# Two stacked transformer blocks with experts: the row sums of an expert move between the next expert's gate and up products, the sums signal by halves, the next layer's weights wait for them, and the last norm reads PSUM

## The reference, cut to what matters

```
for l in range(DEPTH):                      # DEPTH = 2
    h = rms_norm_2(x, norm1_g[l]) * (1 + scale1) + shift1
    proj = h @ w_in[l] + b_in[l]            # w_in: 1024 x 4880
    ...                                     # mixers, merged
    x = x + gate1 * (merged @ w_out[l])
    h2 = rms_norm_2(x, norm2_g[l]) * (1 + scale2) + shift2
    x = x + gate2 * hierarchical_moe(h2, ...)
return rms_norm_2(x, final_norm_g)

# hierarchical_moe, for each of 32 experts e (weights of 2 MB each):
a = t @ w_gate[e]                           # 1024 x 512
u = t @ w_up[e]                             # 1024 x 512
out = out + (silu(a) * u * combine[:, e]) @ w_down[e]   # 512 x 1024
```

## Time and profile before

| what | value |
|---|---|
| median of 3 runs | 2452.65 us (2448.65 to 2454.6) |
| the profiled execution's own time | 2453.15 us |
| its span on the core | 2451.5 us |
| TensorE busy | 91% of the span |
| VectorE, ScalarE, POOL busy | 44%, 24%, 2% |
| DMA, mean | 265 GB/s over the span |
| chain that ended last | PE 67%, DMA 18%, DVE 10%, ACT 3%, issue 1% |

### The profile page before, as it was taken

How to read it: one execution, slowest core, us unless ns; L and a number is a source line. 1 busy time by engine, 2 the same in 40 slices (tenths; PEclk the granted TensorE clock), 3 DMA queues, 4 the chain that set the end, 5 groups by cost and what they waited for, 6 DMA issues and landing times.

```text
span 2451.5 us, 31925 instructions
## 1 busy us (share of the span) xinstructions
PE 2229.5 (91%) x12988; PEld 1455.5 (59%) x12988; DVE 1085.4 (44%) x2397; ACT 589.0 (24%) x1304; POOL 58.4 (2%) x88
## 2 busy tenths in 40 slices
PE   8999999999999999999998987878799999987776
PEld 7888869946865798467764433333568744433332
DVE  4764458883464688543433222222325342222222
ACT  4331523001243220031622111111314422111111
POOL 0010000001000000002000000000002000000000
PEclk9999999999999999999998999998899989999998
DMA  8221244496933645835248999999843469999996
GB/s 304 103 78 69 86 146 165 175 369 206 330 111 116 230 159 205 338 131 172 103 196 361 427 427 428 427 428 427 337 143 111 201 245 428 427 428 427 428 427 295
DMA packets 141054, 650.66 MB, mean 265 GB/s; under 512 B 6986, under 2 KB 13434, under 8 KB 116320
## 3 DMA queue, kind: packets, MB, share of 16 engines
q1 hardware_dynamic: 138480, 641.47, 66.5%
q0 software_dynamic: 2416, 7.02, 1.2%
HBM read 647.16 MB, written 1.31 MB: 265 GB/s over the span
## 4 chain that ended last, share of the span: by engine, by line
PE 67%; DMA 18%; DVE 10%; ACT 3%; issue 1%; DVEq 0%; ACTq 0%
PE ps L106 64%; DMA wring<-in_w_up 11%; DMA AR<-in_w_up 7%; PE ps L109 3%; DVE wring L129 2%; DVE AR L125 2%; ACT AR L115 1%; DVE AR L129 1%; ACT L115 1%; ACT HT L115 1%; DVE wring L125 1%; DVE AR L120 1%; DVE AR L133 0%; ACT wring L115 0%; DVE XN L121 0%
## 5 line engine op out<-in xcount | busy, mean ns | idle before, releaser
L106 PE MATMUL ps<-HT,wring 128*128 128x256 f32 (+1 forms) x2848 | 532.9, 345 | 5.0 <-DVE wring L125 4.0
L106 PEld LDWEIGHTS ps<-HT,wring 128*128 128x128 f32 x2848 | 467.0, 193 | 63.1 <-issue 6.6
L106 PE MATMUL ps<-wring,AR 128*32 128x512 f32 (+3 forms) x1312 | 334.8, 601 | 16.8 <-DVE AR L125 15.7
L106 PE MATMUL ps<-wring,MN 128*32 128x512 f32 (+1 forms) x1376 | 218.9, 643 | 50.8 <-DMA wring<-in_w_up 38.9
L115 ACT ACTIVATE AR<-ps 128x128 f32<-128x128 f32 (+6 forms) x234 | 94.6, 404 | 707.7 <-PE ps L106 651.7
L106 PEld LDWEIGHTS ps<-wring,AR 128*32 128x32 f32 (+1 forms) x1312 | 132.2, 150 | 172.8 <-issue 171.8
L125 DVE TENSOR_TENSOR AR<-ps,AR 128x512 f32<-128x512 f32 (+4 forms) x200 | 100.6, 503 | 261.9 <-ACT AR L115 164.3
L106 PE MATMUL ps<-AR 128*128 128x128 f32 (+6 forms) x1368 | 198.5, 414 | 13.4 <-DVE AR L125 11.0
L106 PEld LDWEIGHTS ps<-wring,MN 128*32 128x32 f32 (+1 forms) x1376 | 66.5, 124 | 194.2 <-issue 103.3
L141 DVE COPY HT<-ps 128x512 f32<-128x512 f32 x64 | 44.3, 692 | 301.1 <-PE ps L106 301.1
L106 PEld LDWEIGHTS ps<-AR 128*128 128x128 f32 (+4 forms) x1368 | 137.1, 176 | 49.8 <-issue 37.4
(11 more groups left out here) (176 smaller groups left out, 2146.3 us busy)
## 6 DMA issues: line engine op xcount, KB each, us to landing
wring<-in_w_up SPq DMA_DIRECT2D x40, 2048.0 KB, 40.8
wring<-in_w_gate SPq DMA_DIRECT2D x38, 2048.0 KB, 41.3
wring<-in_w_down SPq DMA_DIRECT2D x38, 2048.0 KB, 45.4
wring<-in_w_ada SPq DMA_DIRECT2D x24, 2048.0 KB, 11.8
wring<-in_ffn_w_up SPq DMA_DIRECT2D x20, 2048.0 KB, 8.1
AR<-in_w_down SPq DMA_DIRECT2D x20, 2048.0 KB, 45.4
AR<-in_w_gate SPq DMA_DIRECT2D x20, 2048.0 KB, 36.8
wring<-in_w_in SPq DMA_DIRECT2D x18, 2048.0 KB, 10.0
```

What stands on the lines that cost most here:

```text
L106: return Ins(self.eng and self.eng.matmul(out, lhs, rhs, start=start, stop=stop), None)
```

## The change

Four edits, all in the second block.

1. **Order in an expert.** `scatter(ex - 1)` stands between the gate and the up product of `ex`, no longer behind both. `up` is split for that. The fold of the gate's rows signals by itself (`tg`), and the buffer of these rows is freed by that signal.
2. **The sums signal by halves.** The last scatter signals after m = 0 (`first`) and after m = 1 (`end`). `after_join` no longer waits for `join_mm`; `summed(e, layer, m)` waits for the half that the next operation reads.
3. **Weights of layer 1.** SP waits for the end of layer 0's last scatter before it issues `qk1`, and so before all that stands behind it; `qk0` is issued as before.
4. **The last norm.** ScalarE squares both halves of a row straight from PSUM (`final_root`), VectorE adds them, makes the factor and scales from PSUM into `X` (`final_part`); the copies to `X` and VectorE's own square are gone. SP stores four pieces of 256 KB, each as soon as its half is scaled.

```
@@ sync
+                if layer and name == "qk1":
+                    e.wait_ge(sig("join_mm0"), "end")
                 weights((name, layer), win[:, c0:c0 + n], 8, n)
...
         for m in range(2):
-            e.wait_ge(sig("last_v"), ("final", m, 1))
-            e.dma_start(out[0, 128 * m:128 * m + 128, :], X[:, m, :]).then_inc(dma("out"))
+            for c in range(2):
+                h = slice(512 * c, 512 * c + 512)
+                e.wait_ge(sig("last_v"), ("final", m, c))
+                e.dma_start(out[0, 128 * m:128 * m + 128, h], X[:, m, h]).then_inc(dma("out"))
@@ tensor
...
             for ex in range(32):
-                up(ex)
+                up("gate", ex)
                 if ex:
                     scatter(ex - 1)
+                up("eup", ex)
                 inner(ex)
...
-                if ex == 31:
-                    ins.then_inc(sig(f"join_mm{layer}"), "end")
+                    if ex == 31:
+                        ins.then_inc(sig(f"join_mm{layer}"), "end" if m else "first")
@@ vector
+        def final_part(m):
+
+            done, act = sig("norm_v"), sig("norm_a")
+            tag = ("final", m)
+            r, y, z, f = sm((*tag, "r"), 2), sm((*tag, "y"), 1), sm((*tag, "z"), 1), sm((*tag, "f"), 1)
+            v.wait_ge(act, (*tag, "square", 1))
+            v.tensor_scalar(r[:, 1:2], r[:, 1:2], 1e-6, None, ADD).then_inc(done, (*tag, "sum"))
+            v.wait_ge(act, (*tag, "square", 0))
+            v.tensor_tensor(f, r[:, 0:1], r[:, 1:2], ADD).then_inc(done)
+            v.wait_ge(act, (*tag, "root"))
+            v.reciprocal(z, y).then_inc(done)
+            v.scalar_tensor_tensor(f, z, f, z, MUL, MUL).then_inc(done)
+            v.tensor_scalar(f, f, -0.5, 1.5, MUL, ADD).then_inc(done)
+            v.tensor_tensor(f, z, f, MUL).then_inc(done)
+            v.wait_ge(dma("fn"), "final")
+            for c in range(2):
+                h = slice(512 * c, 512 * c + 512)
+                v.scalar_tensor_tensor(X[:, m, h], PA[("moe", 1), m, c][:, :], f, MG[:, h], MUL, MUL).then_inc(sig("last_v"), (*tag, c))
@@ scalar
             table()
             for m in range(2):
+                summed(a, layer, m)
                 tag, key = ("moe", layer), (sig("norm_a"), ("last", layer, m))
+                if layer:
+                    final_root(m)
+                    continue
...
+        def final_root(m):
+
+            done = sig("norm_a")
+            tag = ("final", m)
+            r, y = sm((*tag, "r"), 2), sm((*tag, "y"), 1)
+            for c in (1, 0):
+                a.activation(XN[:, m, c * 512:c * 512 + 512], PA[("moe", 1), m, c][:, :], ACT.Square, scale=1.0 / 32,
+                             accum_out=r[:, c:c + 1]).then_inc(done, (*tag, "square", c))
+            a.wait_ge(sig("norm_v"), (*tag, "sum"))
+            a.activation(y, r[:, 0:1], ACT.Sqrt, bias=r[:, 1:2]).then_inc(done, (*tag, "root"))
@@ all
     def after_join(e, layer):
 
-        for name in ("mm", "v", "a"):
+        for name in ("v", "a"):
             e.wait_ge(sig(f"join_{name}{layer}"), "end")
+
+    def summed(e, layer, m):
+
+        e.wait_ge(sig(f"join_mm{layer}"), "end" if m else "first")
```

More of the change, by code:

```diff
@@ L1443, in moe @@
             after_join(e, layer)
+            summed(e, layer, 1)
         def gather(layer, p):
@@ L1478, in sparse, with up @@
             _, HG, SWT, GC, UC, AT, YS, _ = moe_rings(layer)
-            def up(ex):
+            def up(name, ex):
                 p, x = ex // 2, ex % 2
@@ L1483, in up @@
                 e.wait_ge(vect, ("g", p))
-                for name in ("gate", "eup"):
-                    wx = weights((name, layer, ex), 8, 512)
-                    ps = bank(e, PB, (name, ex))
-                    for i in range(2):
-                        for q in range(4):
-                            k = 2 * q + i
-                            ins = e.matmul(ps[32 * q:32 * q + 32, :], HG[p][:, k, 32 * x:32 * x + 32], wx[:, k, :], i == 0, i == 1)
-                    ins.then_inc(read, (name, ex))
-                    W.free((name, layer, ex), (read, (name, ex)))
+                wx = weights((name, layer, ex), 8, 512)
+                ps = bank(e, PB, (name, ex))
+                for i in range(2):
+                    for q in range(4):
+                        k = 2 * q + i
+                        ins = e.matmul(ps[32 * q:32 * q + 32, :], HG[p][:, k, 32 * x:32 * x + 32], wx[:, k, :], i == 0, i == 1)
+                ins.then_inc(read, (name, ex))
+                W.free((name, layer, ex), (read, (name, ex)))
             def inner(ex):
                 ps = bank(e, PB, ("t", ex))
-                for n, (tile, ready) in enumerate(((GC[ex], (act, ("gate", ex))), (UC[ex], (vect, ("eup", ex))))):
+                for n, (tile, ready, key) in enumerate(((GC[ex], (act, ("gate", ex)), ("tg", ex)), (UC[ex], (vect, ("eup", ex)), ("t", ex)))):
                     e.wait_ge(*ready)
@@ L1501, in inner @@
                         ins = e.matmul(ps[:, c:c + 32], tile[:, f, :], C("fold", 32), True, True)
-                ins.then_inc(done, ("t", ex))
+                    ins.then_inc(done, key)
             def lower(ex):
@@ L2130, in last_part @@
                 h = slice(512 * c, 512 * c + 512)
-                v.scalar_tensor_tensor(X[:, m, h], X[:, m, h], r, (MG if tag == "final" else MF)[:, h], MUL, MUL).then_inc(sig("last_v"), (tag, m, c))
+                v.scalar_tensor_tensor(X[:, m, h], X[:, m, h], r, MF[:, h], MUL, MUL).then_inc(sig("last_v"), (tag, m, c))
+        def final_part(m):
[15 more added lines that the diff above has]
+                v.scalar_tensor_tensor(X[:, m, h], PA[("moe", 1), m, c][:, :], f, MG[:, h], MUL, MUL).then_inc(sig("last_v"), (*tag, c))
         def nsa():
@@ L2432, in moe @@
             for m in range(2):
+                if layer:
+                    final_part(m)
+                    continue
+                summed(v, layer, m)
                 v.tensor_copy(X[:, m, 512:1024], PA[tag, m, 1][:, :]).then_inc(sig("last_v"), (tag, m, 1))
                 PA.free((tag, m, 1), (sig("last_v"), (tag, m, 1)))
-                if layer == 0:
-                    norm_part(("mix", 1), m)
-                else:
-                    last_part("final", m)
+                norm_part(("mix", 1), m)
         def picked(x, m, p):
@@ L2989, in moe @@
             for m in range(2):
+                summed(a, layer, m)
                 tag, key = ("moe", layer), (sig("norm_a"), ("last", layer, m))
+                if layer:
+                    final_root(m)
+                    continue
                 a.activation(X[:, m, 0:512], PA[tag, m, 0][:, :], ACT.Copy).then_inc(*key)
                 PA.free((tag, m, 0), key)
-                norm_root("final" if layer else ("mix", 1), m, key)
+                norm_root(("mix", 1), m, key)
             if layer == 0:
@@ L3022, in sparse @@
                 PB.free(("gate", ex), (done, ("gate", ex)))
-                GC.free(ex, (mm, ("t", ex)))
+                GC.free(ex, (mm, ("tg", ex)))
                 key = (sig(f"join_a{layer}"), "end") if ex == 31 else (done, ("silu", ex))
```

2 lines of the change are left out of this document (1 added, 1 removed).

## The result

| what | before | after |
|---|---|---|
| median of 20 runs | 2456.58 us (2448.65 to 2461.48) | 2448.56 us (2444.18 to 2450.63) |
| ratio after / before, 95% interval | | 0.997 [0.9963, 0.9978] |
| span of the profiled execution | 2451.5 us | 2447.1 us |

The ratio is worth 7.4 us (5.4 to 9.1), and the medians differ by 8.0; 8.3 was forecast. The ratio lies on the edge of 0.3% that the prediction named, and not clearly beyond it. The three runs of before on which the forecast stood had a median 3.9 us under that of the 20 runs here, so the forecast time (2444.4) is low by more than the forecast gain is off; the measured time is inside the range of 2441 to 2449.

The account below looks back on a forecast made before the run. Weight loads were taken to bound the expert stages. Gains of 3.9 us at layer 0's join and 4.4 at the end sum to 8.3, taking the profiled 2453.15 us to 2444.85, median 2444.4; range 2441 to 2449.

Parts of the forecast that it names:

- What bounds, and that nothing inside an expert counts.: Expert stages: weight loads, 14.5 us per expert against TensorE's 12.2, set the pace; only stage ends, join and program end count.
- the rival of TensorE as the bound: Expert stages: new waits make an expert longer than 14.5 us; at 3 us more per expert, 2490 us; chance 0.03.
- Layer 1 has the same durations and I take the same.: End of layer 1's expert stage: the earlier scatter gains the same 1.65 us as at layer 0's end.
- scatter ahead of up: Last expert of each layer: silu comes 1.9 us earlier, but the down weights' landing limits the gain to 1.65 us.
- a low clock at one end: Last expert of one layer: its 7.8 us become 14 at a lower granted clock; gain 2.1, 2450.6 us; chance 0.1.
- For the other experts I cost the edit at nothing.: All experts but the last: slack of 14.5 against 12.2 us covers the new waits; 58 us at worst without it.
- Held weights: Join of layer 0: a nearly empty queue shortens the instruction fetch; gain 3.9 us, including 1.65 from the order.
- The sum's halves: Join of layer 0: signalling by halves gives nothing by itself; the first half is ready before any engine has its code.
- The last norm: End of layer 1: the norm straight from PSUM ends at 2444.5 instead of 2448.33; gain 3.8 us, 1.6 from the order.
- ScalarE sets the tail: Program end, rival: ScalarE's instruction fetch takes 5.3 us; gain 6.3, 2446.4 us; chance 0.1.
- The smaller store: Program end: a last store of 256 KB instead of 512 saves 0.6 us.
- The sum: Whole kernel: 3.9 at layer 0's join plus 4.4 at the end makes 8.3 us, bounds 3.9 and 9.5.

Follow-up runs that it names:

- order_only: The kernel before with only the scatter moved between gate and up and the gate rows' fold signalling by itself: 2453.31 us, ratio 0.999.
- hold_all: The changed kernel with SP's wait one load earlier, ahead of `qk0` instead of `qk1`: 2448.42 us, ratio 0.997 to the kernel before.
- fill_three: The changed kernel with filler products in the routing, at the start of layer 1's mixer and ahead of expert 31's gate weights: 2444.79 us, ratio 0.9957 to before.
- fill_last: The changed kernel with five filler products ahead of the gate weights of expert 31 in both layers: 2448.27 us, ratio 0.9977 to the kernel before.
- hold_from_v: The changed kernel with SP's wait one load later, ahead of `v` instead of `qk1`: 2452.38 us, ratio 0.9995 to the kernel before.
- hold_only: The kernel before with only the hold of layer 1's later weights until layer 0's last scatter: 2454.43 us, ratio 0.9997.
- norm_only: The kernel before with only the sums signalling by halves and the new last norm with its 256 KB stores: 2454.9 us, ratio 1.0004.
- old_order: The changed kernel with the old order in an expert restored, scatter behind gate and up: 2448.31 us, ratio 0.9982 to the kernel before.

## Why the prediction was right, and where it was not

- **What bounds, and that nothing inside an expert counts.** Right: the plateaus stand, folds wait 0.2 us in all for copies, and the rival of TensorE as the bound did not come.
- **"Layer 1 has the same durations and I take the same."** This is the step that failed, and with it the term of 1.65 us for *scatter ahead of up* in each layer. It took every product of expert 31 at 1.92 us. Measured from the landing of the last up weights to the end of the weighting, layer 1 gained 0.4 us in one profile (order_only) and lost 0.2 to 0.7 in four, among them both of the changed kernel, because the gate product of expert 31 ran 3.1 to 3.5 us and its down product 3.2 to 3.6 us. Layer 0 gained 1.6 us in three profiles of five and 0.1 to 0.2 in the other two. Over whole stages the order's two terms come to between nothing and 0.4 us, for 3.3 forecast.
- **What the clock follows there.** The new order lets TensorE wait 0.8 to 1.4 us for the down weights right before the down product; the old order had it wait 0.8 for VectorE. That wait isn't enough to tell: behind 0.99 us the product took 1.92 in layer 0 of hold_all and 3.60 in layer 1 of fill_three. In the kernels without fillers the slow gate product of layer 1 stood behind a wait of 2.1 to 3.0 us. What sets the clock there in the end stays open. fill_last shows that with all products at 1.92 the 1.65 are there (7.63 for 9.30). The rival *a low clock at one end* had this mechanism, but at a chance of 0.1, and priced it at 6 us on four products; it struck one or two, and cost 1.2 to 1.7 us each.
- **"For the other experts I cost the edit at nothing."** From first load to the last gate weights' landing it is 418.5 us in the new order for 418.2 in the old on average, which is within the spread of the profiles.
- **Held weights.** The mechanism was right, the size too small. Without the order's part, 2.25 us were forecast and 2.8 measured (2.4 to 2.8 over the five held kernels without fillers): VectorE came back 2.35 us after its weighting, not 2.97, about as soon as in layer 1. hold_from_v shows what decides: not how many loads are queued, but whether the queue has run down when the engines jump. TensorE's own fetch was covered, and in the changed kernel no product waited for `in_w_in`.
- **The sum's halves.** In layer 0 nothing by themselves, as forecast: the join is 8.75 us in hold_only and 8.76 in the changed kernel. At the end of layer 1 they let ScalarE start its squares some 0.8 us before the scatter's end; the prediction's chain for the last norm has that in it.
- **The last norm.** 2.24 us for 2.2 forecast; from weighting to last scaling 8.51 us for 8.52. *ScalarE sets the tail* did not come: 2.20 us of issue before the table load.
- **The smaller store.** 0.25 us in the changed kernel and 0.4 in norm_only, for 0.6: from the last scaling to the span's end the last 512 KB took 3.2 to 3.4 us and the last 256 KB 2.8 to 3.0. Most of that time didn't shrink with the bytes.
- **The sum.** With the hold, the norm and the store as measured in their places it is 2.8 + 2.24 + 0.25 = 5.3 us, and 5.3 to 5.7 with the order by whole stages, for 8.3; the times give 7.4 (5.4 to 9.1), so these terms lie at the low end of the interval, and about 2 us of the gain are found in no place. How much of it the order has isn't settled: order_only's 0.999 and the step from 0.9982 to 0.997 both speak for 2.5 to 3 us, with intervals that reach down to nothing, while the medians of old_order and the changed kernel are equal. That the forecast gain came out near the measured one is in part luck: the order's terms were too high by some 3 us and the hold's too low by 0.5, and the rest lies in what no profile places.

## What to carry to other kernels

A jump into code that isn't there yet costs according to what the DMA queues hold at that moment. Here that was 5.1 to 5.3 us behind running loads and 2.2 to 3.0 where they had run down. Look at who jumps when, and hold back the loads that nobody needs yet until the jump is over: all but what the first product needs, and even that load if it can land behind the other work of the join. When an order is changed, price a product behind a new wait at both clocks: here it took 3.2 to 3.6 us in 8 of 18 stages and 1.92 in the others. And an edit of 2 or 3 us is read from its own place in several profiles, not from the times of one edit alone.

## What the hardware showed that was not expected

- With one load thinning out or none in flight, ScalarE's pause at the jump was 2.2 to 3.0 us; with two loads or the whole queue it was 5.1 to 5.3. No profile has a value between. The first packet of the instruction queue moved 0.6 to 1.2 us after ScalarE's last operation in the one case and 3.3 to 3.4 in the other (kernels without fillers).
- Five filler products around the two masks and the gather, which do nothing, go with 0.2% less time than the changed kernel's (0.997 to 0.995), of which the profile places 4.6 us at the two routings: the gather went from 3.68 to 1.94 us, that is from a granted clock of 0.50 (1.2 GHz) to 1.00 (2.4 GHz).
- The same fillers at the join left it at 8.9 us in one profile and at 10.9 to 11.0 in two others, through a pause of 2.36 and 2.45 us of "issue" in the midst of straight code. Whether that is a fetch, and why it came in these two, stays open.
